# A transformer pair in split fp32: three SBUF buffers moved to multiples of 2048 bytes

## The chip, the cores and the metric

The kernel runs on one core of a Trainium2 chip. The metric is the time on the device in microseconds, from the start to the end of one execution; the time shown is the median of three runs.

## What is computed

Two transformer blocks, one after the other, on one sequence of 512 tokens with 1024 features. Reduced to what matters here:

```python
# first block
h = rms_norm(x, g_pre_mix) * (1 + sc1) + sh1          # sc1, sh1, ... from c @ w_ada + b_ada
proj = h @ w_in                                       # all heads' q, k, v, index and gate columns
o = concat(nsa_attention(...), dsa_attention(...))    # compressed, selected and windowed attention
x = x + gt1 * rms_norm(o @ w_out, g_post_mix)
x = x + gt2 * rms_norm(relu(h2 @ w_up)**2 @ w_down, g_post_ffn)
# second block
x = x + 0.5 * swiglu(rms_norm(x), ffn1_gate, ffn1_up, ffn1_down)
p = rms_norm(x) @ w_in_2
x = x + concat(stick_breaking_attention(p), rwkv7_time_mix(p)) @ w_out_2
x = x + 0.5 * swiglu(rms_norm(x), ffn2_gate, ffn2_up, ffn2_down)
```

All arrays are float32.

## The kernel before

The features lie on the 128 partitions; x is 8 tiles of 512 tokens (2048 bytes in each partition). Every large matrix product is done in split precision: the weights and the activations are each cut into a high part, rounded to the float32r format, and a low part, the rest. `product` (lines 361 to 365) issues three matmuls for each pair of tiles: high by high (line 363), high by low (364), low by high (365). The first argument is the stationary tile of 128 columns, the second the moving tile, mostly of 512 columns. The profile names the moving tile first: `bank<-hs,wsp` moves hs over the weights wsp.

Weights come as a stream of tiles (`STREAM`, line order written out by hand): a DMA of the SyncE queue brings a tile into `ring` (4 buffers), ScalarE rounds it into the high half of `wsp` (line 1086), VectorE subtracts to get the low half (line 1561), and `take` lets TensorE wait for that. `wsp` has 3 buffers of two halves of 1408 columns, 5632 bytes each.

The activations' two parts stand in these tiles:

- `hs`, 2 x 8 tiles of 512 columns: the input of w_in, w_up, the gate and up products and w_in_2.
- `hids`, 2 x 11 tiles, at the start of `arena`: the hidden values that w_down, down1 and down2 multiply.
- `h2a`, `orw`, `oalt`: chunks that find no room in hs and lie in the arena. `h2_at` gives h2a for the first four chunks and hs for the last four, `mixed_at` hs for the first four and orw for the last, `out_at` oalt for the first three and hs for the rest.

Two products move the weights and hold the activations: w_v (slices of 348 columns, `token_gemm`, 2 tiles of 4 slices) and w_v2 (slices of 512 columns, 4 tiles of 2 slices). Line 364 there moves the low half of wsp, lines 363 and 365 the high half. `arena` is one buffer of 75,776 bytes that all stages share; its tiles begin at multiples of 1024 or of 512 bytes from its start. `hal` and `wal` are views of hs and wsp that other stages use as room. Products in plain float32, without the split, are those of the norms (lines 413 to 423), the adaptation (433), attention scores and small stages.

Buffers are placed by hand. `at` (line 152) puts each at the next free multiple of 64 bytes from 16896 on. The order of the calls therefore sets where each begins:

| buffer | begins at, before | beyond a multiple of 2048 | after the change | beyond a multiple of 2048 |
|---|---|---|---|---|
| x | 16896 | 512 | 18432 | 0 |
| hs | 33280 | 512 | 34816 | 0 |
| ring | 66048 | 512 | 67584 | 0 |
| wsp | 88576 | 512 | 90112 | 0 |
| cst | 122368 | 1536 | 123904 | 1024 |
| tmp | 137152 | 1984 | 138688 | 1472 |
| arena, hids | 149440 | 1984 | 151552 | 0 |
| oalt, orw, h2a | arena + 18432, + 16384, + 45056 | 1984 | the same | 0 |

The order of instructions on each engine is written out by hand, and semaphores order the engines; none of that hangs on addresses.

Of the kernel before, what the change touches and what calls it, by code (L numbers as in the profile page):

```python
# [9 lines left out]
F32R = mybir.dt.float32r  # L10
# [5 lines left out]
P = 128  # L16
T = 512
D = 1024
KD = D // P
NT = T // P  # L20
# [9 lines left out]
CMP_N = 32  # L30
CMP_L = 32
CHUNK = 64
NCH = T // CHUNK
# [68 lines left out]
NG = FF2 // P // 2  # L102
# [34 lines left out]
def build(nc, xt, consts, cols, pos, ada, ada_late, mats, extra, out):  # L137
    ctx = ExitStack()
    with ctx:
# [10 lines left out]
        place = [SBUF_START]  # L150

        def at(name, shape, dt=F32, offset=None):

            size = 4 * int(np.prod(shape[1:]))
            if offset is None:
                offset = place[0]
                place[0] += (size + 63) // 64 * 64
            return nc.alloc_sbuf_tensor_at(name, shape, dt, offset=offset), offset

        x, _ = at("x", [P, KD, T])  # L160

        hs, hs_at = at("hs", [P, 2, KD, T], F32R)
        hal, _ = at("hal", [P, 2 * KD * T], F32, hs_at)
        ring, _ = at("ring", [P, RING, SLOT])
        wsp, wsp_at = at("wsp", [P, SPLIT, 2, SLOT], F32R)
        wal, _ = at("wal", [P, SPLIT * 2 * SLOT], F32, wsp_at)
        cst, _ = at("cst", [P, NCONST])
        col, _ = at("col", [P, NCOLS])
        ext, _ = at("ext", [P, 2 * T + 2 * DH])
        tmp, _ = at("tmp", [P, 6, T])  # L170
        arena, arena_at = at("arena", [P, 74 * 256])
        hids, _ = at("hids", [P, 2, NG, T], F32R, arena_at)
        mod, _ = at("mod", [P, 48])
        gain, _ = at("gain", [P, 32])
        gates, _ = at("gates", [P, NT, 24])
        widx, _ = at("widx", [P, NT, 4])
        best8, _ = at("best8", [P, 8])
        smin, _ = at("smin", [P, 4])
        ssum, _ = at("ssum", [P, 4])
        coef, _ = at("coef", [P, HEADS])  # L180
        hidc, _ = at("hidc", [P, 2, 2, CMP_N])
        rsum, _ = at("rsum", [P, 4])
        coef2, _ = at("coef2", [P, HEADS])
        cmin, _ = at("cmin", [P, HEADS])
        epsc, _ = at("epsc", [P, 3])
        sbg, _ = at("sbg", [P, 2])
        omka, _ = at("omka", [P, 4])
        ends, _ = at("ends", [P, 4, NCH])
        c32, _ = at("c32", [P, KD, 32])
        ropein, ropet, relu_t = tmp[:, 0:2, :], tmp[:, 2:4, :], tmp[:, 4:6, :]  # L190
        bank = ctx.enter_context(nc.psum_tensor("bank", [P, 8, T], F32))

# [37 lines left out]
        oalt, _ = at("oalt", [P, 16, T], F32R, arena_at + 4 * 18 * K)  # L230
# [20 lines left out]
        orw, _ = at("orw", [P, 2, 4, T], F32R, arena_at + 4 * 16 * K)  # L251
        h2a, _ = at("h2a", [P, 2, 4, T], F32R, arena_at + 4 * 44 * K)
# [2143 lines left out]
```

## Time and profile before

| | |
|---|---|
| median of 3 runs | 1938.95 us (1936.39 to 1939.06) |
| profiled execution | 1930.27 us |
| its span, first to last instruction | 1928.5 us |
| mean granted TensorE clock | 0.986 |
| TensorE busy in the span | 1834.7 us, 95% |
| VectorE, ScalarE, GpSimd busy | 936.6, 697.7, 135.5 us |

The span is what the rows of the trace cover; 1.77 us of the profiled execution lie around it. A matmul's row shows its start and a duration; matmuls overlap in the engine, and their ends are modelled, so the pace is read as the distance from one start to the next. Granted clock is the share of full speed that the chip gave TensorE.

### The profile page before, as it was taken

Reading aid. Unit: us, or ns where it says so; the run is one execution under the profiler, and the core shown is the slowest. Engines: PE = TensorE matmul, PEld = TensorE weight load, DVE = VectorE, ACT = ScalarE, POOL = GpSimd, SP = SyncE. Lnnn points to the kernel's source line nnn. Section 1 sums busy time; section 2 is a strip of 40 time slices with the busy share of each in tenths; the row PEclk is TensorE's granted clock in tenths of the full one; section 3 lists DMA queues with packets and bytes.
Section 4 is the critical chain, followed back from the end, with each engine's and each line's share of the span. In section 5 each row is a group of like instructions: output and inputs, shape, how many; then the busy total and the mean of one; then the engine's idle time right before and its main releaser. Section 6 shows DMA issues by size and latency. Waiting matters only on the chain.

```text
span 1928.5 us, 27690 instructions
## 1 busy us (share of the span) xinstructions
PE 1834.7 (95%) x11652; PEld 1414.4 (73%) x11652; DVE 936.6 (49%) x1482; ACT 697.7 (36%) x1055; POOL 135.5 (7%) x109
## 2 busy tenths in 40 slices
PE   5999989989999998999999999899988899999999
PEld 2666655768888886788888877555778678888887
DVE  5277886363434344544244444445754644434442
ACT  4225557242323133332133334577311533312320
POOL 0023444200000002000000010000000110000000
PEclk8999999989999999999999999999999999999999
DMA  9662101212222222223223212111000222322231
GB/s 379 259 246 88 50 12 34 87 45 99 95 91 99 98 93 83 76 94 119 72 99 108 100 66 86 56 38 39 24 4 4 77 97 89 127 70 88 99 126 39
DMA packets 44476, 176.15 MB, mean 91 GB/s; under 512 B 5569, under 2 KB 5825, under 8 KB 41025
## 3 DMA queue, kind: packets, MB, share of 16 engines
q1 hardware_dynamic: 44352, 174.38, 25.5%
q8 instruction: 93, 1.52, 0.3%
q14 instruction: 31, 0.25, 0.0%
HBM read 168.33 MB, written 2.10 MB: 88 GB/s over the span
## 4 chain that ended last, share of the span: by engine, by line
PE 85%; DVE 7%; DMA 3%; ACT 3%; issue 2%; SPq 0%; DVEq 0%; ACTq 0%
PE bank L363 24%; PE bank L364 23%; PE bank L365 23%; PE bank L507 2%; DMA arena<-ada_late 1%; PE bank L523 1%; PE bank L539 1%; PE bank L714 1%; PE bank L855 1%; DMA arena<-ada 1%; PE bank L872 1%; PE bank L863 1%; DMA ring<-m_w_v 1%; ACT wsp L1086 1%; DVE arena L2051 1%
## 5 line engine op out<-in xcount | busy, mean ns | idle before, releaser
L1561 DVE TENSOR_TENSOR wsp<-ring,wsp 128x1024 fp32r<-128x1024 f32 (+2 forms) x244 | 312.9, 1284 | 445.5 <-ACT wsp L1086 445.4
L363 PE MATMUL bank<-hs,wsp 128*128 128x512 f32 x1160 | 472.1, 407 | 16.0 <-DVE hs L1828 5.3
L1086 ACT ACTIVATE wsp<-ring 128x1024 fp32r<-128x1024 f32 (+2 forms) x244 | 268.7, 1103 | 597.4 <-PE bank L365 590.2
L364 PE MATMUL bank<-hs,wsp 128*128 128x512 f32 x1160 | 454.6, 392 | 0.0
L365 PE MATMUL bank<-hs,wsp 128*128 128x512 f32 x1160 | 453.8, 391 | 0.0
L363 PEld LDWEIGHTS bank<-hs,wsp 128*128 128x128 f32 x1160 | 218.9, 189 | 87.4 <-issue 30.7
L364 PEld LDWEIGHTS bank<-hs,wsp 128*128 128x128 f32 x1160 | 219.3, 189 | 49.7 <-issue 6.0
L365 PEld LDWEIGHTS bank<-hs,wsp 128*128 128x128 f32 x1160 | 219.1, 189 | 47.2
L365 PE MATMUL bank<-hids,wsp 128*128 128x512 f32 x608 | 239.6, 394 | 0.0
L363 PE MATMUL bank<-hids,wsp 128*128 128x512 f32 x608 | 239.6, 394 | 0.0
L364 PE MATMUL bank<-hids,wsp 128*128 128x512 f32 x608 | 239.6, 394 | 0.0
L364 PEld LDWEIGHTS bank<-hids,wsp 128*128 128x128 f32 x608 | 113.7, 187 | 28.2
L363 PEld LDWEIGHTS bank<-hids,wsp 128*128 128x128 f32 x608 | 113.7, 187 | 28.1
L365 PEld LDWEIGHTS bank<-hids,wsp 128*128 128x128 f32 x608 | 113.7, 187 | 28.1
L2192 POOL TENSOR_TENSOR arena<-arena 128x512 f32<-128x512 f32 x24 | 41.2, 1718 | 1182.0 <-ACT arena L1098 1182.0
L1886 DVE SCALAR_TENSOR_TENSOR x<-bank,x 128x512 f32<-128x512 f32 x40 | 27.7, 692 | 151.4 <-PE bank L365 151.4
L1292 ACT ACTIVATE hids<-tmp 128x512 fp32r<-128x512 f32 x44 | 27.8, 633 | 118.3 <-DVE tmp L1876 118.3
L363 PE MATMUL bank<-h2a,wsp 128*128 128x512 f32 x176 | 69.8, 396 | 0.0
L364 PE MATMUL bank<-h2a,wsp 128*128 128x512 f32 x176 | 69.3, 394 | 0.0
L365 PE MATMUL bank<-h2a,wsp 128*128 128x512 f32 x176 | 69.3, 394 | 0.0
L1199 ACT ACTIVATE arena<-arena,smin 128x512 f32<-128x512 f32 (+3 forms) x96 | 53.0, 556 | 24.1 <-DVE smin L1730 23.9
L1289 ACT ACTIVATE tmp<-tmp 128x512 f32<-128x512 f32 x44 | 27.8, 632 | 85.2 <-DVE tmp L1870 85.2
(340 smaller groups left out, 2107.5 us busy)
## 6 DMA issues: line engine op xcount, KB each, us to landing
ring<-m_gate SPq DMA_DIRECT2D x44, 512.0 KB, 3.4
ring<-m_up SPq DMA_DIRECT2D x44, 512.0 KB, 3.4
ring<-m_down SPq DMA_DIRECT2D x32, 704.0 KB, 4.0
ring<-m_w_in SPq DMA_DIRECT2D x38, 512.0 KB, 3.5
arena<-ada_late SPq DMA_DIRECT2D x16, 1024.0 KB, 7.0
ring<-m_w_up SPq DMA_DIRECT2D x32, 512.0 KB, 3.4
ring<-m_w_down SPq DMA_DIRECT2D x32, 512.0 KB, 3.4
ring<-m_w_out SPq DMA_DIRECT2D x16, 512.0 KB, 3.6
```

The lines of the kernel that those rows point to most:

```text
L363: pe.matmul(out, lhs[0], rhs[0], start=start, stop=False)
L364: pe.matmul(out, lhs[0], rhs[1], start=False, stop=False)
L365: return pe.matmul(out, lhs[1], rhs[0], start=False, stop=stop)
L507: pe.matmul(bank[:, b, 0:kv], proj[DH * e:DH * e + DH, (QN, QN, QD)[br] + i, t * P:(t + 1) * P], proj[DH * e:DH * e + DH, (KSL, KW, KDD)[b ...
L523: mm = pe.transpose(bank[:, b, (c + k) * P:(c + k + 1) * P], soft[p % 4][:, e, k * P:(k + 1) * P], const("ident"))
L1086: act.activation(wsp[:, s % SPLIT, 0, 0:size], ring[:, i % RING, 0:size], ACT.Copy)\
L1199: act.activation(soft[p % 4][:, e, 0:kv], soft[p % 4][:, e, 0:kv], ACT.Exp, scale=-1.0, bias=smin[:, n:n + 1], accum_out=ssum[:, n:n + 1]) ...
L1289: act.activation(ftmp[:, n % 2, :], ftmp[:, n % 2, :], ACT.Silu).then_inc(S("silu"), 1)
L1292: act.activation(hids[:, 0, n, :], ftmp[:, n % 2, :], ACT.Copy).then_inc(S("hid2_hi"), 1)
L1561: dve.tensor_tensor(wsp[:, s % SPLIT, 1, 0:size], ring[:, i % RING, 0:size], wsp[:, s % SPLIT, 0, 0:size].bitcast(F32), ALU.subtract).then ...
L1886: dve.scalar_tensor_tensor(out=x[:, nn, :], in0=bank[:, nn % 4, :], scalar=scale, in1=x[:, nn, :], op0=ALU.mult, op1=ALU.add).then_inc(S(" ...
L2192: pool.tensor_tensor(sq_at(tag, 0), sq_at(tag, 0), sq_at(tag, k), ALU.add).then_inc(S("sq_sum"), 1)
```

## The change

Eight small buffers (mod, gain, gates, hidc, ends, widx, best8, smin) move from behind the arena to in front of x, where they take 1536 bytes. A new function `align` rounds the next place up to a multiple of 4 T = 2048 bytes; it is called ahead of hs, of wsp and of the arena. The other small buffers move from behind the arena to in front of it, apart from c32, which stays behind. Nothing else differs: the same instructions in the same order, with other addresses.

```diff
+        def align():
+
+            place[0] = (place[0] + 4 * T - 1) // (4 * T) * (4 * T)
+
+        mod, _ = at("mod", [P, 48])
+        gain, _ = at("gain", [P, 32])
+        gates, _ = at("gates", [P, NT, 24])
+        hidc, _ = at("hidc", [P, 2, 2, CMP_N])
+        ends, _ = at("ends", [P, 4, NCH])
+        widx, _ = at("widx", [P, NT, 4])
+        best8, _ = at("best8", [P, 8])
+        smin, _ = at("smin", [P, 4])
         x, _ = at("x", [P, KD, T])
-
+        align()
         hs, hs_at = at("hs", [P, 2, KD, T], F32R)
         hal, _ = at("hal", [P, 2 * KD * T], F32, hs_at)
         ring, _ = at("ring", [P, RING, SLOT])
+        align()
         wsp, wsp_at = at("wsp", [P, SPLIT, 2, SLOT], F32R)
         wal, _ = at("wal", [P, SPLIT * 2 * SLOT], F32, wsp_at)
         cst, _ = at("cst", [P, NCONST])
         col, _ = at("col", [P, NCOLS])
         ext, _ = at("ext", [P, 2 * T + 2 * DH])
         tmp, _ = at("tmp", [P, 6, T])
-        arena, arena_at = at("arena", [P, 74 * 256])
-        hids, _ = at("hids", [P, 2, NG, T], F32R, arena_at)
-        mod, _ = at("mod", [P, 48])
...
         omka, _ = at("omka", [P, 4])
-        ends, _ = at("ends", [P, 4, NCH])
+        align()
+        arena, arena_at = at("arena", [P, 74 * 256])
         c32, _ = at("c32", [P, KD, 32])
+        hids, _ = at("hids", [P, 2, NG, T], F32R, arena_at)
```

## Rows read from the trace of the kernel before

**Rows 1.** Page: busy us (share) xinstructions, and granted clock in 40 slices.

```profile
PE 1834.7 (95%) x11652; PEld 1414.4 (73%) x11652; DVE 936.6 (49%) x1482; ACT 697.7 (36%) x1055; POOL 135.5 (7%) x109
...
PEclk8999999989999999999999999999999999999999
```

**Rows 2.** Chain that ended last: shares of the span by line.

```profile
by line: PE bank L363 23.5%; PE bank L364 23.2%; PE bank L365 23.2%; PE bank L507 1.6%; issue 1.5%; DMA arena<-ada_late 1.5%; PE bank L523 1.4%; PE bank L539 1.4%; PE bank L714 1.1%; PE bank L855 0.9%; DMA arena<-ada 0.9%; PE bank L872 0.8%
```

**Rows 3.** Page, groups: xcount | busy us, mean ns | idle us before, releaser.

```profile
L363 PE MATMUL bank<-hs,wsp 128*128 128x512 f32 x1160 | 472.1, 407 | 16.0 <-DVE hs L1828 5.3
...
L363 PEld LDWEIGHTS bank<-hs,wsp 128*128 128x128 f32 x1160 | 218.9, 189 | 87.4 <-issue 30.7
...
L363 PE MATMUL bank<-hids,wsp 128*128 128x512 f32 x608 | 239.6, 394 | 0.0
```

**Rows 4.** Groups by line and form, TensorE, same columns.

```profile
L363 PE MATMUL bank<-h2a,wsp 128*128 128x512 f32 x176 | 69.8, 396 | 0.0
...
L413 PE MATMUL bank<-arena,cst 128*128 128x512 f32 x48 | 27.2, 691 | 4.9 <-ACT arena L1098 4.9
...
L433 PE MATMUL bank<-arena,c 128*32 128x512 f32 x176 | 23.5, 623 | 19.7 <-DMA arena<-ada 14.3 <-DMA arena<-ada_late 5.4
...
L363 PE MATMUL bank<-orw,wsp 128*128 128x512 f32 x32 | 12.9, 404 | 5.0 <-DVE orw L2163 5.0
...
L363 PE MATMUL bank<-oalt,wsp 128*128 128x512 f32 x24 | 9.6, 398 | 1.4 <-DVE hs L1752 1.4
```

**Rows 5.** Timeline, TensorE, hids: start us, us; first and last of 105.

```profile
897.73 0.39 PE L363 MATMUL bank<-hids,wsp 128*128 128x512 f32 x1
...
921.99 0.39 PE L365 MATMUL bank<-hids,wsp 128*128 128x512 f32 x1
```

**Rows 6.** Timeline, TensorE, hs: first and last of 107.

```profile
799.75 0.39 PE L363 MATMUL bank<-hs,wsp 128*128 128x512 f32 x1
...
823.77 0.39 PE L364 MATMUL bank<-hs,wsp 128*128 128x512 f32 x1
```

**Rows 7.** Timeline of one GEMM: twelve h2a, twelve hs, the next instruction.

```profile
1556.52 0.39 PE L363 MATMUL bank<-h2a,wsp 128*128 128x512 f32 x1
...
1559.32 0.39 PE L363 MATMUL bank<-hs,wsp 128*128 128x512 f32 x1
...
1562.06 0.59 PE L421 MATMUL bank<-arena,cst 128*128 128x512 f32 x1
```

**Rows 8.** Timeline of w_v2's last tile: first three and the 23rd start.

```profile
1208.08 0.39 PE L363 MATMUL bank<-wsp,hs 128*128 128x512 f32 x1
1208.31 0.39 PE L364 MATMUL bank<-wsp,hs 128*128 128x512 f32 x1
1208.53 0.39 PE L365 MATMUL bank<-wsp,hs 128*128 128x512 f32 x1
...
1213.07 0.39 PE L364 MATMUL bank<-wsp,hs 128*128 128x512 f32 x1
```

**Rows 9.** Waits, ScalarE: us in total, times, longest us.

```profile
ACT wsp L1086 <- PE bank L365: 590.2, 194, 6.7
```

**Rows 10.** Timeline, TensorE, plain fp32 products of 512 columns, merged.

```profile
1496.05 3.70 PE L1040 MATMUL bank<-arena,cst 128*128 128x512 f32 x8 [0.47 <-ACT arena L1477]
1499.58 3.60 PE L1043 MATMUL bank<-arena,ext 128*128 128x512 f32 x8
```

**Rows 11.** DMA issues: xcount, KB each, median us to landing.

```profile
arena<-ada SPq DMA_DIRECT2D x6, 1024.0 KB, 12.5
...
hal<-ada SPq DMA_DIRECT2D x2, 1024.0 KB, 11.5
```

**Rows 12.** Timeline of w_v's second tile: each slice's first of twelve.

```profile
52.80 0.32 PE L363 MATMUL bank<-wsp,hs 128*128 128x348 f32 x1
...
54.68 0.32 PE L363 MATMUL bank<-wsp,hs 128*128 128x348 f32 x1
...
56.57 0.32 PE L363 MATMUL bank<-wsp,hs 128*128 128x348 f32 x1
```

More of the change, by code:

```diff
@@ L170, in build @@
         tmp, _ = at("tmp", [P, 6, T])
-        arena, arena_at = at("arena", [P, 74 * 256])
-        hids, _ = at("hids", [P, 2, NG, T], F32R, arena_at)
-        mod, _ = at("mod", [P, 48])
[L174 to L178, printed above, removed]
         ssum, _ = at("ssum", [P, 4])
         coef, _ = at("coef", [P, HEADS])
-        hidc, _ = at("hidc", [P, 2, 2, CMP_N])
         rsum, _ = at("rsum", [P, 4])
```

## The prediction

> **What bounds the kernel.** I read the page first: TensorE is busy 95% of the span, at nine tenths of its clock or more in nearly every slice, its weight loads 73%, no other engine half [rows 1]. Then the chain that ended last: 70% of it stands on the three lines 363 to 365 of `product` [rows 2]. So the pace of these matmuls sets the time. Last I took the groups of instructions, on the page and by form [rows 3, 4]. The reader is to see that one form, 512 columns of split fp32, makes up nearly all the work, and that its groups differ only in the moving tile: hs 1160 triplets (3,480 matmuls), hids 608, h2a 176, orw 32 and oalt 24 (together 840 triplets, 2,520 matmuls, all of them in the arena), and w_v2, where the split weights move (32 triplets, 96). Their durations have modelled ends, so I do not use them; I take the pace from starts in the timeline. In a long stretch with hids, 105 starts lie between 897.73 and 921.99 us: 24.26 / 104 = 233.3 ns each [rows 5]. With hs, 107 starts between 799.75 and 823.77: 24.02 / 106 = 226.6 ns [rows 6]. Both lie in slices with nine tenths of the clock or more, and each start follows the one before at an even step, so neither waits for another engine.
>
> The difference of 6.67 ns belongs to the moving operand. In one GEMM of the last block the first four chunks move h2a and the next four hs, with one weight tile and one bank: twelve matmuls take 2.80 us (1556.52 to 1559.32, 233.3 ns), the next twelve 2.74 us (228.3 ns) [rows 7]. What differs between the tiles is where they begin: hs 512 bytes past a multiple of 2048, everything in the arena 1984 past one, that is 448 past a multiple of 512, with 64 bytes or 16 columns left to the next.
>
> **The change part by part.**
>
> *The arena to a multiple of 2048.* I expect its 2,520 matmuls to run at the pace of the tiles that begin at a multiple of 512. Which multiple does not matter by the trace: in w_v2 line 364 moves the low part of a weight tile, and in the tile that runs from 1208.08 us this part begins at a multiple of 2048 exactly (88576 + 2 x 11264 + 5632 = 57 x 2048), while lines 363 and 365 move the high part, 512 past one. 23 starts from 1208.08 to 1213.07 give 4.99 / 22 = 226.8 ns, and the steps after lines 363 and 364 are 0.23 and 0.22 us [rows 8]. So phase 0 is worth what phase 512 is. Gain: 2,520 x (233.3 - 226.6) = 16.8 us. It is all on the path: the hids stages have no idle time before a matmul [rows 3], and the cover behind is wide: ScalarE's splits waited 590 us in all for TensorE to free a weight buffer [rows 9], and the hs stages feed the same 128x1024 weight tiles at the faster pace already. The smaller groups orw and oalt (168 matmuls, 1.1 us of the sum) stand partly beside waits [rows 4]; without them the gain is 15.7.
>
> *hs and the split weights to a multiple of 2048.* By the same w_v2 rows phase 512 to phase 0 is worth nothing for a moving operand, and the weight slices of 512 bytes fall on every phase that is a multiple of 512 before and after. Value taken: 0 for 3,576 matmuls. A weight load takes 189 ns [rows 3], inside a pace of 227, so it does not set it.
>
> *fp32 matmuls that move arena tiles* (lines 413 and 433, 224 of 512 columns, are the largest such groups [rows 4]). Where they set the end no such operand lies at another phase, so the trace gives no comparison. Bounds: nothing, or the same 6.67 ns each, 1.5 us. Eight of line 1040 take 3.53 us (1496.05 to 1499.58), 441 ns each, about twice as long for as many columns as a split one [rows 10]; with twice the time for one read a stop of 6.67 ns has room to hide, so I take 0.
>
> *The switch from h2a to hs.* Twelve hs matmuls after h2a take 2.74 us against 2.72 at the steady pace. If all tiles share one phase the 0.02 us may go in 44 GEMMs and 8 more: 0 to 1.0 us. It is two digits of one row; I take 0.
>
> *DMAs into the arena.* The ada loads of 1 MB land in 12.5 us in the arena and in 11.5 in hal, which is a part of hs at a multiple of 512 [rows 11]. These loads are 2.4% of the chain [rows 2], 46 us, so at most 8% of 46, 3.7 us. The six arena loads queue among others and the two hal loads are later ones, so this need not be the address; I take 0.
>
> *VectorE and ScalarE, and the small vectors in front.* Nothing is issued more or less, no wait moves, no queue changes: 0. What the addresses might do to these engines lies behind TensorE, as ScalarE's wait shows [rows 9]; without that cover a change there would count in full.
>
> Sum: -16.8 us. The profiled execution took 1930.27 us, 1.77 beside its span of 1928.5; it would become 1913.5 with a span of 1911.7. That execution was 8.7 under the median of the runs, 1938.95, so I forecast the median 1938.95 - 16.8 = **1922.1 us**. Bounds of this case: 15.7 less to 16.8 + 1.5 + 1.0 + 3.7 = 23.0 less, 1916.0 to 1923.3; the three runs lie within 2.7 us of each other, so 1914 to 1926.
>
> **The rivals.**
>
> *No change (1939).* The pace may hang on the place in the memory and not on the phase: every slow tile lies above byte 149440, every fast one below 122368 (hs 33280, split weights 88576), and no split matmul moves a 512-phase tile up there. For it speaks w_v: there the moving slices of 348 columns, low in memory, begin 0, 1392, 2784 and 4176 bytes past a multiple of 512, and the steps stay level: in the second tile twelve at phase 368 take 1.88 us (52.80 to 54.68, 157 ns), the next twelve at 224 take 1.89 (157 ns) [rows 12]; 348 columns at the pace of hs with its surplus over 512 would be 158. Against it: these slices have 36 and 72 columns before the next multiple of 512, the arena tiles only 16, so a stall that needs a very short first piece would spare them; and the two paces are constant to the digit over stages with different neighbours, which points to a regular cost of the address. Arena stays above byte 149440 after the change, so by this rival all 2,520 keep 233.3 ns: 1938.95. The Trainium skill ("SBUF — State Buffer", Specifications) has 16-byte lines as the unit whose crossing costs; by it a tile at a multiple of 64 is as good as one at 2048, which is this rival; that hs and h2a differ in [rows 7] though both are on such lines is not explained by it.
>
> *Much faster (down to 1841).* A tile within one 2048-byte block might be read without any stop, and hs too would gain. At 2.4 GHz 512 columns take 213.3 ns: 3,576 x 13.3 + 2,520 x 20 = 98 us. The w_v2 rows speak against it: a moving tile within one block runs no faster [rows 8]. The Trainium skill ("TensorE: Matmul & The Clock Gate", Back-to-back issue gap) gives N/2.4 + 2.5 ns, 215.8 here, as the pace of a single matmul after another; by it both groups have something to shed, as an estimate 3,576 x 10.8 + 2,520 x 17.5 = 83 us, 1856. No row here comes near that pace.
>
> *Slower (1963).* With arena and split weights at a common phase, a moving tile and every fourth weight slice begin at the same place modulo 2048. If that made the two reads stop each other for one such step, 6.67 ns, on every split matmul (6,096 beside w_v), it would cost 40.7: 1938.95 - 16.8 + 40.7 = 1963. It decides from 2,520 matmuls on, where it eats the gain; on every fourth alone it would cost 10.2. Against it: hs and the split weights share phase 512 now, and every fourth slice coincides, at the faster pace of [rows 6].
>
> **How the numbers follow.** The phase: 0.72. No change: 0.19. Much faster: 0.04. Slower: 0.05. About 0.2% (3.9 us) is what a measurement of this kernel tells from no change. The first case is faster nearly always, with the third 0.75; same 0.20; slower 0.05. The predicted time is that of the first case. Its own range, 1914 to 1926, leaves out 0.28, so the range reaches over no change: 1914 to 1940.
>
> **What would show it.** Right: 105 starts of a hids stretch in 23.6 us instead of 24.26; h2a and hs at one pace within a GEMM; hs and w_v2 unchanged at 226.6; span near 1911.7, all of the difference in the stages with hids, h2a, orw and oalt. Wrong: hids still at 233.3 (place, not phase); hs below 226 (blocks of 2048 do count); hs or hids at 233 or above with hs before at 226.6 (the two reads meet).

## The result and the profile after

The changed kernel takes 1918.67 us (median of 4 runs, 1914.31 to 1923.62) against 1939.01 in the same comparison; the ratio is 0.989 with a 95% interval of 0.9854 to 0.9927. The profiled execution took 1914.31 us with a span of 1912.5; forecast were 1922.1, 1913.5 and 1911.7. So the medians differ by 20.3 us (14 to 28 by the interval) and the profiled executions by 16.0, where the forecast had 16.8.

The page of the changed kernel, groups of instructions (xcount | busy us, mean ns of one | idle before). All line numbers are 6 higher than before, so 369 to 371 are `product`:

```profile
L369 PE MATMUL bank<-hids,wsp 128*128 128x512 f32 x608 | 236.5, 389 | 0.0
...
L369 PE MATMUL bank<-h2a,wsp 128*128 128x512 f32 x176 | 68.9, 391 | 0.0
```

The modelled durations alone, 389 and 391 ns where [rows 3, 4] had 394 and 396, hint at it; the pace is read from starts. The changed kernel's timeline, TensorE (start us, us, line, tiles):

```profile
339.47 0.50 PE L369 MATMUL bank<-oalt,wsp 128*128 128x512 f32 x1 [1.42 <-DVE hs L1758]
...
450.76 0.39 PE L369 MATMUL bank<-hids,wsp 128*128 128x512 f32 x1
...
894.63 0.39 PE L369 MATMUL bank<-hids,wsp 128*128 128x512 f32 x1
...
919.11 0.39 PE L369 MATMUL bank<-hids,wsp 128*128 128x512 f32 x1
...
1183.87 0.79 PE L369 MATMUL bank<-wsp,hs 128*128 128x512 f32 x1
...
1548.43 0.39 PE L369 MATMUL bank<-h2a,wsp 128*128 128x512 f32 x1
...
1551.15 0.39 PE L369 MATMUL bank<-hs,wsp 128*128 128x512 f32 x1
...
1553.87 0.59 PE L427 MATMUL bank<-arena,cst 128*128 128x512 f32 x1
...
1909.01 0.39 PE L371 MATMUL bank<-hids,wsp 128*128 128x512 f32 x1
```

The hids stretch from 894.63 to 919.11 has 109 starts: 24.48 / 108 = 226.7 ns, where [rows 5] had 233.3. In the GEMM of [rows 7] both halves now take 2.72 us (1548.43 to 1551.15 to 1553.87), so h2a and hs run alike. The other rows are stage starts; the same points in the kernel before, beside the 1556.52 of [rows 7]:

```profile
336.31 0.50 PE L363 MATMUL bank<-oalt,wsp 128*128 128x512 f32 x1 [1.42 <-DVE hs L1752]
...
448.15 0.39 PE L363 MATMUL bank<-hids,wsp 128*128 128x512 f32 x1
...
1190.47 0.79 PE L363 MATMUL bank<-wsp,hs 128*128 128x512 f32 x1
...
1924.96 0.40 PE L365 MATMUL bank<-hids,wsp 128*128 128x512 f32 x1
```

| stretch | before, us | after, us | difference | arena matmuls in it x 6.67 ns |
|---|---|---|---|---|
| start to first oalt | 336.31 | 339.47 | +3.2 | none |
| to first hids | 111.84 | 111.29 | -0.6 | 72: -0.5 |
| to w_v2 | 742.32 | 733.11 | -9.2 | 1,296: -8.6 |
| to first h2a | 366.05 | 364.56 | -1.5 | 96: -0.6 |
| to last hids | 368.44 | 360.58 | -7.9 | 1,056: -7.0 |

From the first oalt on the kernel gains 19.1 us, all in stretches with arena matmuls. The 3.2 us that the profiled execution loses ahead of them is no effect of the addresses that the runs show: the same program, run again, reaches the first oalt at 342.35 us instead of 339.47, and with the arena put back (arena back, below) it comes at 341.95. In the stages ahead of it TensorE's granted clock falls at other moments in each execution. Windows of 60 us there (busy us of TensorE, granted clock, DMA), before and then after:

```profile
150.00:210.00 60.00, 54.31 (x396) 1.00 0.18 59
```

```profile
150.00:210.00 60.00, 54.31 (x364) 0.94 0.18 58
```

TensorE was equally busy and got fewer matmuls done: a mean of 0.94 says that it stood at the lower of its two levels (1.2 and 2.4 GHz) for part of that window. In the second execution of the changed program the same window has 0.91.

### The profile page after: what moved, and what is told of

The parts are those of the page before. It is cut to its first block, busy times and chain, and to the rows that moved or that the text cites. A ratio compares the mean times of both kernels' runs of the same rounds, so it can differ in the third digit from the quotient of the medians.

```text
span 1912.5 us, 27690 instructions
## 1 busy us (share of the span) xinstructions
PE 1820.0 (95%) x11652; PEld 1418.0 (74%) x11652; DVE 935.8 (49%) x1482; ACT 697.6 (36%) x1055; POOL 135.3 (7%) x109
## 4 chain that ended last, share of the span: by engine, by line
PE 85%; DVE 7%; ACT 3%; DMA 3%; issue 2%; SPq 0%; DVEq 0%; ACTq 0%
PE bank L369 24%; PE bank L371 23%; PE bank L370 23%; PE bank L513 2%; PE bank L529 1%; PE bank L545 1%; DMA arena<-ada_late 1%; PE bank L720 1%; PE bank L861 1%; DMA arena<-ada 1%; PE bank L878 1%; PE bank L869 1%; DMA ring<-m_w_v 1%; ACT wsp L1092 1%; DVE arena L2057 1%
## 5 line engine op out<-in xcount | busy, mean ns | idle before, releaser
L369 PE MATMUL bank<-hids,wsp 128*128 128x512 f32 x608 | 236.5, 389 | 0.0
L370 PE MATMUL bank<-hids,wsp 128*128 128x512 f32 x608 | 236.5, 389 | 0.0
L371 PE MATMUL bank<-hids,wsp 128*128 128x512 f32 x608 | 236.5, 389 | 0.0
```

The lines of the kernel that those rows point to most:

```text
L369: pe.matmul(out, lhs[0], rhs[0], start=start, stop=False)
L370: pe.matmul(out, lhs[0], rhs[1], start=False, stop=False)
L371: return pe.matmul(out, lhs[1], rhs[0], start=False, stop=stop)
```

## The experiments

**Which of the three buffers.** Three kernels: the arena alone moved, the changed kernel with the arena put back, and the changed kernel again.

```diff
 # arena alone: the kernel before, with the arena behind the small buffers
-        arena, arena_at = at("arena", [P, 74 * 256])
...
+        place[0] = (place[0] + 4 * T - 1) // (4 * T) * (4 * T)
+        arena, arena_at = at("arena", [P, 74 * 256])
```

```diff
 # arena back: the changed kernel
-        align()
         arena, arena_at = at("arena", [P, 74 * 256])
```

> The arena alone is moved to a multiple of 2048 (151552); hs and the split weights stay 512 past one. If the arena's phase is the whole cause: the time of the changed kernel, ratio to before about 0.991, span near 1912.5, hids at 226.7 ns. If all three buffers must be on multiples of 2048: a part of the gain, ratio 0.995 or nearer 1. If hs and the weights gave some of the gain: slower than the changed kernel by that part.

> The changed kernel without the last rounding up: hs and the split weights at multiples of 2048, the arena at 151488, 1984 past one. Phase theory: hids, h2a, orw and oalt back at 233.3 ns, ratio to before 1.000 within 0.2%, span near 1928.5. Place theory (a gain from something else in the layout): hids stays at 226.7 and the ratio at 0.991.

> The changed kernel once more, beside the two others on the same chip. Every theory: ratio to before 0.989 to 0.993, hids at 226.7 ns.

Measured: arena alone 0.9908 (0.9894 to 0.9923), arena back 1.0005 (0.9989 to 1.0022), changed kernel again 0.9898 (0.9880 to 0.9917). The timelines of the first two, the first of 264 hids matmuls in a row and the hs matmul that follows them:

```profile
899.13 0.39 PE L364 MATMUL bank<-hids,wsp 128*128 128x512 f32 x1
...
958.97 0.39 PE L364 MATMUL bank<-hs,wsp 128*128 128x512 f32 x1
```

```profile
901.53 0.39 PE L368 MATMUL bank<-hids,wsp 128*128 128x512 f32 x1
...
963.13 0.39 PE L368 MATMUL bank<-hs,wsp 128*128 128x512 f32 x1
```

59.84 / 264 = 226.7 ns and 61.60 / 264 = 233.3 ns. The arena's address is the whole effect; moving hs and the split weights from 512 to 0 past a multiple of 2048 is worth nothing that these intervals show.

**The pace by itself.** A kernel of only such matmuls, in the pattern of `product`, with the moving tile at 22 distances low in memory and 11 high; the weights begin at a multiple of 256.

```python
for k in range(7):
    for j in range(3):
        s = (k + j // 2) % 8
        pe.matmul(bank[:, b, 0:width], ws[:, s * P:(s + 1) * P], m[:, 0:width],
                  start=(k + j == 0), stop=(k == 6 and j == 2))
```

> This kernel leaves out all of the reference's work: it loads x, fills tiles and issues split-fp32 matmuls in the kernel's pattern (three with two weight slices, 42 per case) whose moving tile begins at a chosen distance past a multiple of 2048, low in memory (38912 to 129024) and high (from 151552). Phase theory in the form 'a short first piece before a multiple of 512': about 227 ns at distances 0 to 384, rising over 400 to 480 towards 233 or more at 448 (16 columns left), the same low and high, and 448 = 1984 by a multiple of 512. Phase theory in the form 'not a multiple of 128': 233 ns at 64, 192, 320 and 448, 227 at 128, 256 and 384. Place theory: 227 ns at every low distance, 233 at every high one. Theory of blocks of 2048 bytes: only 0 is at the lowest pace. Slices of 348 and 256 columns show whether the surplus is fixed per matmul. Plain fp32 at 0, 64 and 448: equal within 1 ns if half the read rate hides the step, 6.7 ns apart if not.

Its timeline, first row of each case and of the next; 42 matmuls lie between (the name says region and distance; `plain` is fp32 without the split, merged rows):

```profile
139.95 0.39 PE L61 MATMUL bank<-lo256b,w 128*128 128x512 f32 x1
...
149.49 0.40 PE L61 MATMUL bank<-lo320b,w 128*128 128x512 f32 x1
...
207.92 0.39 PE L61 MATMUL bank<-lo448b,w 128*128 128x512 f32 x1
...
217.72 0.40 PE L61 MATMUL bank<-lo464b,w 128*128 128x512 f32 x1
...
333.92 0.39 PE L61 MATMUL bank<-hi448b,w 128*128 128x512 f32 x1
...
343.71 0.39 PE L61 MATMUL bank<-hi512b,w 128*128 128x512 f32 x1
...
438.34 18.19 PE L61 MATMUL bank<-plain0b,wplain 128*128 128x512 f32 x42
456.36 18.19 PE L61 MATMUL bank<-plain64b,wplain 128*128 128x512 f32 x42
474.39 18.19 PE L61 MATMUL bank<-plain448b,wplain 128*128 128x512 f32 x42
```

At 256 a matmul takes 9.54 / 42 = 227 ns. At 448 it takes 233 ns low (9.80 / 42) and 233 high (9.79 / 42). So the place in memory is out, and 256 is as good as 512. All other distances from 16 to 480 lay between 229 and 235 ns, those far ahead of a multiple of 512 too, and 496, with only 4 columns left to it, ran at 227 (237.37 to 246.89 us for 42). That speaks against the form "a short first piece"; 128 at 232 (120.39 to 130.15) speaks against the form "not a multiple of 128". Plain fp32 is indifferent. Its 21 matmuls a case stand in 42 rows, two for each, and a row takes 429 ns at 0 (18.02 / 42) and at 64 (18.03 / 42), so a matmul takes 858.

**In the kernel: 64 and 256, and the weights.** One line is added to the changed kernel in each, `place[0] += 64` or `+= 256` ahead of the arena, or `+= 64` ahead of wsp.

> The changed kernel with the arena 64 past a multiple of 2048. Theory 'a short first piece before a multiple of 512' (112 columns left here): hids stays at 226.7 ns, ratio to before 0.990. Theory 'multiples of 256': hids at 228.9 to 233.3 ns, ratio 0.993 to 1.000.

> The changed kernel with the arena 256 past a multiple of 2048, so no longer at a multiple of 512. Theory 'multiples of 256' and 'a short first piece': 226.7 ns, ratio 0.990. Theory 'multiples of 512 or 2048': 233 ns, ratio about 1.000.

> The changed kernel with the split weights alone 64 past a multiple of 2048; hs and the arena stay on multiples. Theory 'either operand': every split matmul of 512 columns at 233.3 ns, 6096 x 6.67 = 41 us more than the changed kernel, about 1960, ratio 1.011. Theory 'only the moving operand counts': the changed kernel's time but for w_v2's 96 matmuls, ratio 0.990.

Measured: 0.9962 (0.9946 to 0.9977), 0.9926 (0.9902 to 0.9950) and 1.0095 (1.0075 to 1.0115). In the second the 264 hids matmuls run at 226.7 ns (first start 897.85, last 957.46: 59.61 / 263); its gain is a little less than the 0.990 expected, but of the 8.8 us by which its profiled span exceeds that of the changed kernel 4.9 lie ahead of the first oalt and 3.5 between w_v2 and h2a, stretches that differ between executions. The timeline of the first, with the same two points:

```profile
899.67 0.40 PE L370 MATMUL bank<-hids,wsp 128*128 128x512 f32 x1
...
960.11 0.40 PE L370 MATMUL bank<-hs,wsp 128*128 128x512 f32 x1
```

60.44 / 264 = 228.9 ns: 64 past a multiple, with 112 columns left to the next multiple of 512, costs. That is where my reason for the gain falls. And of the third, with the last of the 528 hs matmuls that follow, then the first and the 23rd of w_v2's last tile:

```profile
911.95 0.40 PE L370 MATMUL bank<-hids,wsp 128*128 128x512 f32 x1
...
973.55 0.40 PE L370 MATMUL bank<-hs,wsp 128*128 128x512 f32 x1
...
1096.52 0.39 PE L372 MATMUL bank<-hs,wsp 128*128 128x512 f32 x1
...
1229.16 0.39 PE L370 MATMUL bank<-wsp,hs 128*128 128x512 f32 x1
...
1234.19 0.39 PE L371 MATMUL bank<-wsp,hs 128*128 128x512 f32 x1
```

61.60 / 264 and 122.97 / 527 are both 233.3 ns: with every moving tile on a multiple of 2048, 64 bytes in the weights' address slow all of them. In w_v2 the same two buffers change roles, wsp moves and hs is held, and the pace is another: 5.03 / 22 = 228.6 ns.

**Both addresses.** The kernel of matmuls again, with nine starts of the weights and five of the moving tile past a multiple of 256.

> Leaves out all of the reference's work: split-fp32 matmuls of 512 columns in the kernel's pattern, for nine starts of the weight tile (0 to 240 past a multiple of 256) with five starts of the moving tile. Theory 'both operands at multiples of 256': 226.7 ns only with both at 0 (or 240 for the moving one, as measured before), about 233 with either off, not more with both off. Theory 'each operand costs for itself': 240 with both off. If some pair that is off runs below 226.7 ns, a faster placement exists. The last two cases keep one weight slice for all matmuls: no difference if the loads cost as such, less if a change of the slice costs.

Timeline, first row of each case:

```profile
47.75 0.40 PE L58 MATMUL bank<-moves64b,still0b 128*128 128x512 f32 x1
...
57.38 0.40 PE L58 MATMUL bank<-moves128b,still0b 128*128 128x512 f32 x1
...
67.14 0.39 PE L58 MATMUL bank<-moves192b,still0b 128*128 128x512 f32 x1
...
76.93 0.40 PE L58 MATMUL bank<-moves240b,still0b 128*128 128x512 f32 x1
...
135.75 0.39 PE L58 MATMUL bank<-moves0b,still64b 128*128 128x512 f32 x1
...
145.53 0.39 PE L58 MATMUL bank<-moves64b,still64b 128*128 128x512 f32 x1
...
155.10 0.40 PE L58 MATMUL bank<-moves128b,still64b 128*128 128x512 f32 x1
...
164.73 0.40 PE L58 MATMUL bank<-moves192b,still64b 128*128 128x512 f32 x1
...
174.49 0.40 PE L58 MATMUL bank<-moves240b,still64b 128*128 128x512 f32 x1
```

| moving tile ahead of the weights by (modulo 256) | weights at 0 | weights at 64 |
|---|---|---|
| 0 | 226.7 (9.52 / 42, 38.23 to 47.75 us) | 9.57 / 42 = 227.9 (moves 64) |
| 64 | 9.63 / 42 = 229.3 | 9.63 / 42 = 229.3 (moves 128) |
| 128 | 9.76 / 42 = 232.4 | 9.76 / 42 = 232.4 (moves 192) |
| 192 | 9.79 / 42 = 233.1 | 9.78 / 42 = 232.9 (moves 0) |

Neither theory that I had written down foretold the first row: both tiles 64 off runs as fast as both at 0 (226.7 ns after the first dozen matmuls, which bear the change of case). What counts is the distance between the two, not either address; it has a sign, so the two roles of hs and wsp in the run before, 192 one way and 64 the other, get 233 and 229. 128 and 128, 192 and 192 were the same, 226.7. The distances 32, 96 and 224, with several starts of the weights, all took 233, and 160 took 234, so the pace at 32 does not lie between those at 0 and 64. Keeping one weight slice for all matmuls changed nothing (226.7 and 233.3 at distances 0 and 192).

**The distance, in the kernel.** Two kernels that no rule of absolute multiples could make fast. First all three buffers 64 off; then the kernel before with the weights alone moved, to the arena's 192 past a multiple of 256 (the arena keeps its 192).

```diff
 # all 64 off: the changed kernel
         align()
+        place[0] += 64
         hs, hs_at = at("hs", [P, 2, KD, T], F32R)
...
-        align()
         wsp, wsp_at = at("wsp", [P, SPLIT, 2, SLOT], F32R)
...
         align()
+        place[0] += 64
         arena, arena_at = at("arena", [P, 74 * 256])
```

```diff
 # weights 192 off: the kernel before
+        place[0] += 192
         wsp, wsp_at = at("wsp", [P, SPLIT, 2, SLOT], F32R)
...
+        place[0] += 64
         arena, arena_at = at("arena", [P, 74 * 256])
```

> The changed kernel with hs, the split weights and the arena each 64 past a multiple of 256 (64 past one of 2048). Theory 'the two operands at the same distance past a multiple of 256': hs and hids at 226.7 ns, ratio to before 0.990 as the changed kernel. Theory 'both at multiples of 256' (or of 2048): every split matmul at 233 ns, 41 us more than the changed kernel, ratio about 1.011.

> The kernel before with the split weights alone moved, from a multiple of 256 to 192 past one, the distance of the arena (which stays 192 past one); hs stays at a multiple of 256. Theory 'same distance': the arena's 2,520 matmuls at 226.7 ns (-16.8 us), hs with a moving tile 64 ahead at 228.9 (3,480 x 2.2 = +7.8), w_v2 at 233 (+0.6): -8.4 us, ratio 0.996. Theory 'both at multiples of 256': hs at 233 as well, +23 us, ratio 1.012. Theory 'only the moving operand counts': 1.000.

Measured: 0.9900 (0.9882 to 0.9918) and 0.9962 (0.9946 to 0.9978), both as the theory of distance says. Timelines, with the same three points (264 hids, then 528 hs):

```profile
900.76 0.39 PE L370 MATMUL bank<-hids,wsp 128*128 128x512 f32 x1
...
960.60 0.39 PE L370 MATMUL bank<-hs,wsp 128*128 128x512 f32 x1
...
1080.05 0.39 PE L372 MATMUL bank<-hs,wsp 128*128 128x512 f32 x1
```

```profile
903.10 0.39 PE L365 MATMUL bank<-hids,wsp 128*128 128x512 f32 x1
...
962.96 0.40 PE L365 MATMUL bank<-hs,wsp 128*128 128x512 f32 x1
...
1083.60 0.39 PE L367 MATMUL bank<-hs,wsp 128*128 128x512 f32 x1
```

All 64 off: 226.7 and 226.7 ns, with none of these operands on a multiple of 256. Weights 192 off: the hids tiles, still 192 past a multiple of 256, now run at 59.86 / 264 = 226.7, and hs, not moved at all, at 120.64 / 527 = 228.9.

One thing in these runs goes beyond the steady paces. Where twelve matmuls at one distance alternate with twelve at another, both halves pay: in arena 64 the h2a half takes 2.76 us and the hs half 2.77 in nearly all GEMMs of the last block, though twelve at 228.9 and 226.7 ns would take 2.75 and 2.72. That is part of why its ratio is 0.996.

**Other widths.** The kernel of matmuls with the distances 0 to 192 at eight widths.

> Leaves out all of the reference's work: split-fp32 matmuls as before, with the moving tile 0, 64, 128 and 192 ahead of the weights modulo 256, for widths from 512 to 128 columns; pairs with both tiles at 16, 32 or 96; and weights of 64 columns. Theory 'same distance': 226.7 ns for (32, 32) and (96, 96), about 233 for 32 against 96. If the equal distance is good for every width, 0 is the lowest in each row; from the 256-column cases already measured I expect 0 to be the slowest there. If the surplus of 32 cycles is the weights' own reads, weights of 64 columns run at about 220 ns.

Timeline; the first four rows are pairs at 512 columns, the last four bound the cases of 256 columns with distance 0 and 192:

```profile
46.25 0.39 PE L60 MATMUL bank<-moves32b,still32b 128*128 128x512 f32 x1
...
55.82 0.39 PE L60 MATMUL bank<-moves96b,still96b 128*128 128x512 f32 x1
...
65.38 0.39 PE L60 MATMUL bank<-moves32b,still96b 128*128 128x512 f32 x1
...
75.18 0.39 PE L60 MATMUL bank<-moves192b,still64b 128*128 128x512 f32 x1
...
248.22 0.28 PE L60 MATMUL bank<-moves0b,still0b 128*128 128x256 f32 x1
...
253.25 0.28 PE L60 MATMUL bank<-moves64b,still0b 128*128 128x256 f32 x1
...
263.18 0.28 PE L60 MATMUL bank<-moves192b,still0b 128*128 128x256 f32 x1
...
267.97 0.25 PE L60 MATMUL bank<-moves0b,still0b 128*128 128x192 f32 x1
```

(32, 32) and (96, 96) take 227.9 and 227.6 ns a matmul with the change of case, 226.7 after it; (32, 96) takes 9.80 / 42 = 233.3. But (16, 16), which the theory has at the same pace, took 230 (36.59 to 46.25 us for 42): for starts that are no multiple of 32 an equal distance is not enough. At 256 columns the order turns round: distance 0 takes 5.03 / 42 = 119.8 ns and distance 192 only 4.79 / 42 = 114.0. The distances 64 and 128 lie between (118 and 119). At 320, 192 and 128 columns the distance makes no difference, and at 480, 448 and 384 the paces of one width lie 3 to 4 ns apart in orders of their own. With weights of 64 columns, distance 0 takes 230 ns instead of 226.7, so the surplus over 512 columns' 213.3 (one column a cycle at 2.4 GHz) is not simply the reading of the weights, the one explanation that I had put down.

## Why the prediction was right, and where its reason was not

*The arena's 2,520 matmuls* were forecast from 233.3 to 226.6 ns, 16.8 us. They run at 226.7, and the stretches that hold them gain what their counts say and 2.3 us more, on which below. hs and w_v2 stayed where they were: 106 hs starts between 799.20 and 823.00 us give 226.7 ns, and w_v2's last tile runs at 226.7 too. The step of 6.67 ns and the count were read from rows, and they carry the forecast.

*The reason given for it failed.* The step "448 past a multiple of 512, with 16 columns left to the next", and with it "the pace of the tiles that begin at a multiple of 512", read the moving tile's address by itself. What counts is its distance from the weight tile modulo 256: 192 for the arena before, 0 after. The change fixed the distance because it put both on multiples of 2048. For the choice of address that is luck: with the weights 64 off, an arena on a multiple of 2048 ran at 233.3 ns. The w_v2 rows [rows 8], read as "phase 0 is worth what phase 512 is", are right by this too: both tiles lie on multiples of 256 there.

*hs and the weights at 0*: right, shown by the arena alone (0.9908 against 0.9898 for all three). *Plain fp32 at 0*: right in value, 429 ns a row at either distance. The reading behind it was not: [rows 10] has two rows for each of line 1040's four matmuls, so 441 ns is half a matmul, and the 224 rows of lines 413 and 433 are 112 matmuls. *DMAs at 0*: nothing gained; the arena's ada loads land in 12.7 us after, 12.5 before. The Trainium skill ("DMA: Bandwidth & Descriptors", How a descriptor splits into AXI transactions) lets the first transaction of a descriptor that does not start at a multiple of 256 begin at the boundary below, which costs beats. These loads, whose place in SBUF came to a multiple of 256 by the change, do not show it in their landing.

*The switch from h2a to hs* was taken at 0 with a bound of 1.0 us. It is 0.8: the stretch to the last hids gains 7.9 where its 1,056 matmuls give 7.0, and twelve hs matmuls behind h2a fell from 2.74 to 2.72 us, 0.02 in each of 44 GEMMs. So this term belonged in the sum. Another 1.5 us of the 19.1 in the table (0.6 on the way to w_v2, 0.9 to h2a, some hundredths elsewhere) I have not assigned. They are no more than executions differ by: the stretch to h2a takes 364.2 to 368.4 us in the five profiles with all these matmuls at 226.7 ns (the changed kernel twice, arena alone, arena 256, all 64 off), and the stretch to w_v2 takes 741.35 in arena back against 742.32 in the kernel before.

*The rivals.* "No change" by place in memory: shown wrong by the high and low tiles at 448, both 233. Its support, the level steps of w_v [rows 12], came from slices of 348 columns, and at widths other than 512 the distance acts in other ways. Nor were they level: the slice behind the two shown, from 56.57 us, ran at 160 ns, and the kernel of matmuls has 157 to 160 for four distances at that width. The 16-byte line of the Trainium skill ("SBUF — State Buffer", Specifications) would make tiles at any multiple of 64 equal; the paces 226.7 to 233.3 do not agree. "Much faster": no pair ran below 226.7 ns at 512 columns, so the 215.8 of the Trainium skill ("TensorE: Matmul & The Clock Gate", Back-to-back issue gap) was not reached by the split matmuls. "Slower, because the two reads meet at a common phase": the contrary holds, the common phase is the fast one.

## What to carry to other kernels

Compare the start-to-start pace of matmul groups of one shape, not their durations: two steady paces at the same clock, with no waits, mean that something in the operands differs, and the counts then price it: 16.8 us here, where 19.1 were gained from the first oalt on. For split-fp32 matmuls of 512 columns put the moving and the weight tile at the same distance past a multiple of 256 bytes, that distance being a multiple of 32; common multiples of 256 are the easy way. Measure again for another width or plain fp32: here 256 columns wanted the opposite and plain fp32 did not care.

## What was not expected of the hardware

- The distance of two operands modulo 256, not an address, sets the pace: 226.7, 229, 232 and 233 ns for 0, 64, 128 and 192 bytes. The rule is not complete. Distance 64 gave 233 ns in one case low in memory (91.08 to 100.87 us for 42), 229 in all others, and distance 128 gave 233.3 with the weights at 128, 232.4 in all others; a moving tile 240 ahead of weights at 0 gave 227 in one run and 236 in another; both tiles at 240 gave 233 and both at 16 gave 230 though their distance is 0. How the stream stood when the case began, and starts that are no multiple of 32, seem to count as well; I have not tried it further, and what in the chip makes the distance count is open.
- A matmul of 256 columns is faster at distance 192 than at 0 (114 against 120 ns).
- At distance 0 the widths 256, 320, 384 and 512 take 120.0, 146.7, 173.3 and 226.7 ns: 0.417 ns, one cycle of 2.4 GHz, for each column, and a fixed 13.3 ns. Why that surplus remains at the best distance of 512 columns stays open: it is there with one weight slice for all matmuls, and weights of half the columns do not lower it.
